# State products of a chunked scan in three reduced passes instead of one plain float32 product

## The reference

```python
acs = jnp.cumsum(da_c, axis=1)
lmat = jnp.exp(jnp.where(causal, seg, -jnp.inf))        # seg = acs_t - acs_s
cb = jnp.einsum('btgn,bsgn->btsg', c_c, b_c)
y = jnp.einsum('btsgh,bsghp->btghp', cb[..., None] * lmat, xdt_c)
y = y + jnp.einsum('btgn,bghpn->btghp', c_c, h) * jnp.exp(acs)[..., None]
decay_to_end = jnp.exp(acs[:, -1:] - acs)
h_new = h * jnp.exp(acs[:, -1])[..., None, None] + jnp.einsum(
    'bsgn,bsghp->bghpn', b_c, xdt_c * decay_to_end[..., None])
```

## Time and profile before

| | |
|---|---|
| median of 3 runs | 1562.04 us (1558.72 to 1562.12) |
| profiled execution, span | 1557.9 us |
| PE busy | 1474.0 us, 95% |
| DVE busy | 700.1 us, 45% |
| ACT busy | 454.9 us, 29% |
| POOL busy | 187.9 us, 12% |

### The profile page before, as it was taken

The page is one execution under the profiler, slowest core; times in us unless marked ns, Lnnn a source line. Parts: engine busy times, 40 slices in busy tenths (PEclk is TensorE's granted clock), DMA queues, the critical chain, the costliest instruction groups (busy, mean ns, idle before and its releaser), DMA issues.

```text
span 1557.9 us, 35095 instructions
## 1 busy us (share of the span) xinstructions
PE 1474.0 (95%) x14547; PEld 1192.0 (77%) x14547; DVE 700.1 (45%) x1304; ACT 454.9 (29%) x875; POOL 187.9 (12%) x360
## 2 busy tenths in 40 slices
PE   8999999999999999999999999989977897898987
PEld 7999999999998999999988879875534443444442
DVE  5766576676789663223354435684111111111114
ACT  4533635353422362213243343211100010010102
POOL 1100000000000000000000000003423232333323
PEclk9999999999999999999999999999999899999989
DMA  5232434544458422262266372959999999999996
GB/s 208 69 94 82 133 109 158 150 124 123 128 208 321 137 82 95 82 227 90 82 201 216 130 304 70 387 205 395 419 423 421 423 420 422 413 404 420 421 422 239
DMA packets 89411, 368.28 MB, mean 236 GB/s; under 512 B 14096, under 2 KB 37856, under 8 KB 75328
## 3 DMA queue, kind: packets, MB, share of 16 engines
q1 hardware_dynamic: 82992, 356.86, 60.5%
q0 software_dynamic: 6144, 8.95, 1.6%
q10 hardware_dynamic: 144, 0.52, 0.1%
HBM read 344.82 MB, written 29.31 MB: 240 GB/s over the span
## 4 chain that ended last, share of the span: by engine, by line
PE 77%; DMA 14%; DVE 5%; issue 1%; ACT 1%; SPq 0%; POOLq 0%; POOL 0%; DVEq 0%; ACTq 0%
PE ps L679 37%; DMA arena<-in_w 14%; PE ps L1229 10%; PE ps L823 6%; PE ps L1248 5%; PE ps L932 3%; PE ps L913 3%; PE ps L1076 1%; PE ps L774 1%; PE ps L771 1%; PE ps L1212 1%; PE ps L943 1%; PE ps L966 1%; PE ps L1016 1%; PE ps L764 1%
## 5 line engine op out<-in xcount | busy, mean ns | idle before, releaser
L1229 PE MATMUL ps<-arena,xT 128*32 128x256 f32 x4096 | 258.8, 406 | 58.4 <-DMA arena<-in_w 57.8
L1229 PEld LDWEIGHTS ps<-arena,xT 128*32 128x32 f32 x4096 | 133.1, 116 | 159.7 <-issue 49.7
L1789 DVE TENSOR_TENSOR wl<-raw,wh 128x1024 fp32r<-128x1024 f32 x151 | 183.4, 1222 | 151.6 <-ACT wh L1320 151.1
L679 PE MATMUL ps<-xh,wh 128*128 128x272 f32 x1136 | 243.4, 295 | 1.4 <-ACT tmp L1332 0.7
L679 PE MATMUL ps<-xh,wl 128*128 128x272 f32 x1136 | 235.0, 288 | 0.0
L679 PE MATMUL ps<-xl,wh 128*128 128x272 f32 x1136 | 234.3, 288 | 0.0
L679 PEld LDWEIGHTS ps<-xh,wh 128*128 128x128 f32 x1136 | 179.1, 188 | 11.8 <-issue 10.0
L679 PEld LDWEIGHTS ps<-xl,wh 128*128 128x128 f32 x1136 | 178.4, 188 | 0.0
L679 PEld LDWEIGHTS ps<-xh,wl 128*128 128x128 f32 x1136 | 177.4, 189 | 0.0
L1320 ACT ACTIVATE wh<-raw 128x1024 fp32r<-128x1024 f32 x151 | 158.0, 1055 | 35.8 <-DMA raw<-in_slabs 19.2
L2578 DVE TENSOR_TENSOR hbuf<-sg,ps 128x128 f32<-128x128 f32 x64 | 18.5, 288 | 295.6 <-ACT sg L1641 295.5
(11 more groups left out here) (463 smaller groups left out, 2363.2 us busy)
## 6 DMA issues: line engine op xcount, KB each, us to landing
arena<-in_w SPq DMA_DIRECT2D x92, 2048.0 KB, 36.6
raw<-in_slabs SPq DMA_DIRECT2D x151, 512.0 KB, 4.4
bc<-acs_dram SPq DMA_DIRECT2D x16, 512.0 KB, 6.0
hs<-in_h SPq DMA_DIRECT2D x16, 512.0 KB, 5.2
out_h_sample<-hs SPq DMA_DIRECT2D x16, 512.0 KB, 3.5
kv<-in_kT SPq DMA_DIRECT2D x8, 1024.0 KB, 4.8
arena<-in_w SPq DMA_DIRECT2D x16, 512.0 KB, 8.1
kvx<-in_vc SPq DMA_DIRECT2D x2, 2048.0 KB, 10.0
```

The source lines that it names most:

```text
L679: r = nc.tensor.matmul(ps[:, 2 * (ub % 2) + half, 0:HT], w[:, s, col], x[:, koff + kk, half * HT:half * HT + HT], start=first and kk == 0 ...
L1229: r = nc.tensor.matmul(ps[QS * c:QS * c + QS, 2, 0:2 * FQ], xT[:, s, kk % 2, kk // 2 * QS:kk // 2 * QS + QS], arena[:, at_:at_ + 2 * FQ], ...
L1789: v.tensor_tensor(wl[:, s], raw[:, s], wh[:, s].bitcast(F32), ALU.subtract).then_inc(w_lo, 1)
```

## The change

The state product is made like the units, from high and low parts of both operands. ScalarE's copy of B into `btok` rounds to the reduced type, VectorE makes `btok_l` by a subtraction; ScalarE makes `xdtd_h` by a new copy of xdtd, and VectorE `xdtd_l`, in place, by another subtraction. xdtd itself is computed before Mt instead of behind it. ScalarE's new copy stands in `decays(it + 1)`, between the exponential of Ef and the Relu's; in the last step, where there are no decays, it stands behind the btok copy. To free semaphores for the two new ones, two pairs in the expert router are merged (`srt_mm` into `rank_mm`, `cur_ov` into `cur`); the order of the work there is the same.

```diff
-        bc = place("bc", [P, 2, HG, P], F32, r_m + 8192)
+        bc = place("bc", [P, 2, HG, P], F32, r_m + 9216)
...
-        btok = place("btok", [P, NS], F32, s0 + 8192)
+        xdtd_l = place("xdtd_l", [P, HG * HD], F32R, s0 + 6144)
+        btok = place("btok", [P, NS], F32R, s0 + 8192)
+        btok_l = place("btok_l", [P, NS], F32R, s0 + 19456)
...
+        xdtd_h = place("xdtd_h", [P, HG * HD], F32R, r_m + 7168)
...
                 pe.wait_ge(xdtd_ready, it + 1)
-                nc.tensor.matmul(ps[:, 4, :], btok[:], xdtd[:], start=True, stop=True).then_inc(pe_b, 1)
+                for n_, (w, x) in enumerate(((btok, xdtd_h), (btok_l, xdtd_h), (btok, xdtd_l))):
+                    r = nc.tensor.matmul(ps[:, 4, :], w[:], x[:], start=n_ == 0, stop=n_ == 2)
+                r.then_inc(pe_b, 1)
...
                     nc.scalar.activation(Ef[:, e % 2], Ef[:, e % 2], ACT.Exp)
+                if it:
+                    act.wait_ge(xdtd_v, it)
+                    nc.scalar.activation(xdtd_h[:], xdtd[:], ACT.Copy).then_inc(xdtd_hi, 1)
                 act.wait_ge(bc_in[it % 2], 16 * (it // 2 + 1))
...
                 if it + 1 < STEPS:
                     decays(it + 1)
+                else:
+                    act.wait_ge(xdtd_v, STEPS)
+                    nc.scalar.activation(xdtd_h[:], xdtd[:], ACT.Copy).then_inc(xdtd_hi, 1)
                 split(b + 2)
...
                 c_.done(v.tensor_tensor(cbm[:], ps[:, 5, 0:P], tri, ALU.mult))
+                c_.sync()
+                v.tensor_tensor(as8(xdtd[:]), as8(xdt[:]), of8(dte_tok), ALU.mult).then_inc(xdtd_v, 1)
+                dve.wait_ge(btok_ready, it + 1)
+                c_.done(v.tensor_tensor(btok_l[:], ps[:, 6, 0:P], btok[:].bitcast(F32), ALU.subtract))
                 dve.wait_ge(mexp, it + 1)
                 c_.sync()
                 v.tensor_tensor(Mt[:, s], Mt[:, s], cbm[:].unsqueeze(1).to_broadcast([P, HG, P]), ALU.mult).then_inc(mready, 1)
-                v.tensor_tensor(as8(xdtd[:]), as8(xdt[:]), of8(dte_tok), ALU.mult).then_inc(xdtd_ready, 1)
+                dve.wait_ge(xdtd_hi, it + 1)
+                v.tensor_tensor(xdtd_l[:], xdtd[:], xdtd_h[:].bitcast(F32), ALU.subtract).then_inc(xdtd_ready, 1)
                 low(b + 2)
```

## The result

| | before | after | ratio, 95% interval |
|---|---|---|---|
| first comparison, 5 runs each | 1562.04 us (1558.72 to 1562.77) | 1566.65 us (1565.76 to 1573.81) | 1.0045 (1.0031 to 1.0058) |
| second comparison, 5 of after, 23 of before | 1561.43 us | 1566.49 us (1565.01 to 1568.65) | 1.0033 (1.0020 to 1.0046) |

The change costs 4.6 and 5.1 us by the medians, 7.0 and 5.2 by the ratios. The forecast was 1566.0. Both intervals lie above 1: the slowdown is small but clear of the noise.

What follows compares the result with a forecast made beforehand. TensorE, busy 235.33 of 236 us, was taken to bound the scan. Terms -4.2 + 1.8 + 4.8 + 0.4 + 0.7 + 0.5 = +4.0 us gave 1566.0 against the median 1562.0; range 1563 to 1568.5, with rivals 1557.5 to 1570.

Steps and rivals of the forecast that it cites:

- state product: TensorE in the scan: three reduced passes for one plain product save 0.28 us in 15 steps, -4.2 us.
- step 0: Scan's first step, already waiting for the evacuation: ScalarE's copy of 0.53 is paid, +0.5 us.
- c = 1: Second step of each four-step group: transposes wait 0.45 us for VectorE's last add, four steps, +1.8 us.
- c = 2: Third step of each group: late Ef delays the evacuation, second unit waits 1.2 us, four steps, +4.8 us.
- c = 3: Fourth step of each group, no Ef: late xdtd makes the evacuation slightly late, four steps, +0.4 us.
- c = 0: First step of each group: copy and later Ef give waits of 0.2, 0.5 and 0 us, +0.7 us.
- Rival A: Extra work stays beside TensorE in the scan and only step 0 pays: -3.7 us, 1558.3; chance 0.13.
- C: Scan's reduced passes cost 0.39 us each, so TensorE loses 3 us: +6.3 us in all, 1568.3; chance 0.05.
- D: VectorE and SP recover between scan steps, waits come to some 4 us, gain and loss cancel: 1562; chance 0.17.
- rival B: Ef transfer takes 5.3, not 4.7 us in each c = 2, its longest in c = 0: +7.2 us, 1569.2; chance 0.2.

Runs made afterwards that it cites:

- first profile: Profiled execution of the changed kernel, the slowest of its five: span 1571.8 us, device time 1573.81, scan 247.13 us against 234.73 before.
- again: Second profiled execution of the unedited changed kernel: span 1564.1 us, device time 1566.16, scan 239.18 us against 234.73 before.
- a3: Changed kernel with the plain state product in place of the three passes (numbers wrong): 1567.50 us against 1561.43 before, ratio 1.0038.
- a4: Changed kernel with GpSimd instead of ScalarE copying xdtd into xdtd_h: 1560.99 us against 1561.43 before, ratio 1.0000.
- b1: Changed kernel with Ef fetched as soon as its buffer is free: 1561.80 us against 1561.10 before, ratio 1.0005.
- a1: The changed kernel run once more, no edit: 1566.49 us against 1561.43 before, ratio 1.0033.
- a2: Kernel before with only its plain state product replaced by three reduced passes over one rounded pair: 1558.84 us against 1561.43 before, ratio 0.9984.
- b2: Changed kernel with ScalarE's copy behind the split of slab b+2 and xdtd_l behind its low part: 1570.77 us against 1561.10 before, ratio 1.0054.
- b3: Changed kernel with a second, unused ScalarE copy of 384 columns beside the first: 1573.06 us against 1561.10 before, ratio 1.0079.
- c3: Changed kernel with ScalarE's copy and xdtd_l placed later and Ef fetched early: 1560.91 us against 1562.21 before, ratio 0.9994.
- b4: Changed kernel with GpSimd making the xdtd_h copy and Ef fetched early: 1560.48 us against 1561.10 before, ratio 0.9991.

## Why the prediction was right, and which terms were not

The scan's difference from before, split by the same terms (waits counted at TensorE's marks):

| term, us | forecast | first profile | again |
|---|---|---|---|
| state product (14 steps fall into the scan as measured) | -4.2 | -2.2 | -2.2 |
| step 0 | 0.5 | 0.5 | 0.5 |
| c = 1, transposes behind the last add | 1.8 | 1.0 | 1.0 |
| c = 2, second unit | 4.8 | 6.5 | 3.1 |
| c = 3 | 0.4 | 0 | 0.3 |
| c = 0 | 0.7 | 2.9 | 1.1 |
| first matmul after a wait, 0.08 each | 0 | 0.6 | 0.6 |
| lower clock | 0 | 3.1 | 0 |
| sum | 4.0 | 12.4 | 4.4 |
| scan, measured | | 12.4 | 4.5 |

- **The mechanism was right.** TensorE bound the scan and had no wait; the copy ahead of the Relu's shifted ScalarE's list by 1.5 us in c = 1; conv_a carried it to the last add (+13.95 against a forecast of +14.02); the fetch of Ef carried it into c = 2. a3 and a4 show that the copy in ScalarE's list is the cause, b1 that the transfer is its larger path. Rival A fell with a1, C with a2. D had the waits come to some 4 us; by the table they are 6.6 us in the second profile, nearer to the forecast's 8.2.
- **State product:** mis-sized. The forecast took 0.28 a step, and named 0.20 as the saving if going from plain to reduced products costs something. It does: the first pass takes 0.33 instead of 0.227. Measured 0.16, less than that too. The forecast's 4.2 also holds a step that the scan's length leaves out. The rule of the Trainium skill (FP8 and Floating Point Precision, TensorE Precision Notes) that plain float32 is four passes would have given 0.23 a step; a2's steps show 0.16, less than that too, and the rule says nothing of the change between kinds.
- **c = 1:** the add came as forecast, but TensorE was due at +13.75, not +13.62, for it had saved less, so the wait was 0.25 (0.3 with its first matmul), not 0.45.
- **c = 2 and c = 0:** the forecast used the transfer times of one execution, 4.7 us on average in c = 2. From the last add to ScalarE's exponential they were 4.8, 5.9, 6.2 and 4.1 in the first profile and 4.8, 4.0, 4.5 and 4.3 again; for the steps with c = 0 they were 6.5, 5.4 and 5.1, and 4.1, 5.4 and 5.0 again, against 4.6, 5.0 and 4.2 in the kernel before. Where the transfer took the 4.8 us (step 2 of both profiles) the wait was the forecast's 1.2. Before, this scatter ended in ScalarE's idle time and nobody saw it; the change put it on the path. That is rival B, and in the first profile it was what happened: c = 2 and c = 0 together 9.4 us against 8.7 in B, 5.5 in the forecast. The medians lie nearer to the forecast.
- **The clock:** absent from the forecast. It made 3.1 us of the first profile and nothing of the second.
- The forecast compared with a median that it took to be 4.1 us over the span; the span's own offset is 2.0 us. This moved nothing, since only the difference counts.
- **What a measurement can tell:** the forecast took 0.3% as the limit and gave 0.56 to no change that can be told and 0.36 to a slowdown. The intervals reach 0.13% to either side, and both tell the slowdown from no change: that limit was set too wide.

That +4.0 and the medians' +4.6 and +5.1 are so close is partly luck: a gain taken 1.8 us too large against waits that in these executions were smaller or larger than the forecast's. Why the transfer takes 4.0 us in one step and 6.5 in another was not tried and stays open.

## What to carry to other kernels

An instruction added to an in-order list brings its wait with it; ask what stands behind both, and where that list's deadlines are, all of them (b2). If a fetch is triggered by the end of work that you delay, its latency follows into the next step, and a transfer that ended in idle time before has to be judged by its slowest, not its mean. Put such a copy on an idle engine and start the fetch when its buffer is free: with both, the same three passes took 2.2 us off the scan. The whole time came out 0.6 and 1.7 us under that of the plain product by the medians, instead of 5 over; the intervals of that comparison just reach 1.

## What the runs showed of the hardware

- A reduced pass of 128x512 starts 0.227 us after the one before, but the second pass starts 0.335 after the first where that stands behind the plain Y products (in all 16 steps): 0.11 more. A unit's second matmul is 0.08 late in the same way behind the plain products of the old state. Both are changes from plain to reduced products. In the other direction the Y products start 0.09 late behind a unit, but they also change the tile form (128*64), and the transposes start with no delay behind one; so no run shows a cost for that direction by itself.
- TensorE's granted clock fell to 1.2 GHz, for about 3.4 us each time, around or just behind waits of 2.11 and 2.40 us (first profile), 1.78 (b3), 2.04, 2.30 and 1.88 (b2) and 2.05 (c3); behind those of 1.62 us in step 4 of the first profile, 1.45 in b3 and shorter ones it did not. So the "over 2 us" of a1's expectation is too high. With the lower clock the waits of 2.11 and 2.40 us made their steps 3.8 and 4.2 us longer.
- GpSimd's copy of 128x512 took 0.62 us, as long as ScalarE's 0.63. VectorE's Mt product, which overlaps it from step 1 on, took 1.44 to 1.45 us instead of 1.23 in all 15 of these steps of b4; in step 0, where the two do not overlap, it took 1.23:

```profile
188.26 0.62 POOL L1710 CAST xdtd_h<-xdtd 128x512 fp32r<-128x512 f32 x1 [16.07 <-DVE xdtd L1944]
188.50 1.45 DVE L1949 TENSOR_TENSOR Mt<-Mt,cbm 128x1024 f32<-128x1024 f32 x1
```
